# Chunk inverses of RWKV and gated delta with 32x32 diagonal blocks in four tiles of TensorE

## What is computed

```python
for i in range(DEPTH):
    xp = macaron_half(xp, *fa); xs = macaron_half(xs, *fa)
    up, us = rmsnorm(xp, norm_w[i, 1]), rmsnorm(xs, norm_w[i, 1])
    mp, ms = mixer(up), mixer(us)         # rwkv, attention, gated delta, rwkv
    xp = xp + mp; xs = xs + ms
    xp = macaron_half(xp, *fb); xs = macaron_half(xs, *fb)
```

```python
a_mat = bc[..., :, None] * einsum('nbhid,nbhjd->nbhij', kc, kc) * decay_strict + eye(L)
sol = triangular_solve(a_mat, rhs, lower=True, unit_diagonal=True)
```

## Time and profile before

| | |
|---|---|
| time, median of 3 runs | 3211.21 us (3207.57 to 3213.80) |
| the profiled execution | 3219.08 us |
| its span, first to last instruction | 3216.4 us |
| mean granted TensorE clock | 0.955 |
| PE busy | 3070.2 us, 95% of the span |
| DVE busy, ACT busy | 1532.2 us, 1066.7 us |
| FFN products, L799 to L801, six groups | 837 + 832 + 829 + 416 + 415 + 414 us |
| Y and X steps of RWKV, L1049 and L1070 | 53.4, 74.2 and 64.1 us |
| Y and X steps of gated delta, L1634 and L1658 | 13.0 and 18.9 us |

### The profile page before, as it was taken

The page is one execution under the profiler, slowest core; times in us unless marked ns, Lnnn a source line. Parts: engine busy times, 40 slices in busy tenths (PEclk is TensorE's granted clock), DMA queues, the critical chain, the costliest instruction groups (busy, mean ns, idle before and its releaser), DMA issues.

```text
span 3216.4 us, 63024 instructions
## 1 busy us (share of the span) xinstructions
PE 3070.2 (95%) x28286; PEld 2761.8 (86%) x28286; DVE 1532.2 (48%) x2422; ACT 1066.7 (33%) x1595; POOL 163.8 (5%) x266
## 2 busy tenths in 40 slices
PE   7998999999999899999999899999999999999998
PEld 6995788799999776699999767789999957887997
DVE  4644343355565204365565453446556435443554
ACT  3432232244443213244443232224344322322432
POOL 1000002100000101000000000400000000021000
PEclk9999999899999997899999899899999989997999
DMA  6442401253554634254643432155454513012532
GB/s 220 152 152 84 141 29 33 53 183 125 189 162 133 214 131 156 65 164 134 192 150 125 161 106 84 43 155 160 153 172 142 172 69 115 29 33 53 173 126 69
DMA packets 333441, 402.32 MB, mean 125 GB/s; under 512 B 14746, under 2 KB 287295, under 8 KB 332813
## 3 DMA queue, kind: packets, MB, share of 16 engines
q1 hardware_dynamic: 320176, 353.20, 33.9%
q0 software_dynamic: 13072, 46.30, 4.9%
HBM read 384.90 MB, written 14.57 MB: 124 GB/s over the span
## 4 chain that ended last, share of the span: by engine, by line
PE 92%; DVE 4%; ACT 2%; issue 1%; DMA 0%; POOL 0%; DVEq 0%; ACTq 0%; POOLq 0%
PE bank L799 18%; PE bank L801 17%; PE bank L800 17%; PE bank L832 10%; PE bank L1381 4%; PE bank L1070 2%; PE bank L908 2%; PE bank L794 2%; PE bank L868 1%; PE bank L884 1%; PE bank L1049 1%; PE bank L1023 1%; PE bank L1154 1%; PE bank L1112 1%; ACT work L1853 1%
## 5 line engine op out<-in xcount | busy, mean ns | idle before, releaser
L799 PE MATMUL bank<-h_hi,w_hi 128*128 128x288 f32 x2816 | 837.2, 297 | 5.8 <-DVE h_lo L2164 5.5
L800 PE MATMUL bank<-h_hi,w_lo 128*128 128x288 f32 x2816 | 831.5, 295 | 0.0
L801 PE MATMUL bank<-h_lo,w_hi 128*128 128x288 f32 x2816 | 828.6, 294 | 0.0
L2172 DVE TENSOR_TENSOR w_lo<-ring,w_hi 128x2048 fp32r<-128x2048 f32 (+1 forms) x304 | 611.0, 2011 | 424.3 <-ACT w_hi L1791 424.3
L1791 ACT CAST w_hi<-ring 128x2048 fp32r<-128x2048 f32 (+1 forms) x304 | 511.1, 1683 | 636.9 <-PE bank L801 568.6
L799 PEld LDWEIGHTS bank<-h_hi,w_hi 128*128 128x128 f32 x2816 | 528.3, 188 | 7.9 <-DVE w_lo L2172 6.0
L801 PEld LDWEIGHTS bank<-h_lo,w_hi 128*128 128x128 f32 x2816 | 531.0, 189 | 0.0
L800 PEld LDWEIGHTS bank<-h_hi,w_lo 128*128 128x128 f32 x2816 | 529.3, 188 | 0.6
L799 PE MATMUL bank<-hid_hi,w_hi 128*128 128x288 f32 x1408 | 416.1, 296 | 0.0
L800 PE MATMUL bank<-hid_hi,w_lo 128*128 128x288 f32 x1408 | 415.4, 295 | 0.0
L801 PE MATMUL bank<-hid_lo,w_hi 128*128 128x288 f32 x1408 | 414.3, 294 | 0.0
(11 more groups left out here) (516 smaller groups left out, 3454.2 us busy)
## 6 DMA issues: line engine op xcount, KB each, us to landing
ring<-in_ffn_w_gate SPq DMA_DIRECT2D x88, 1024.0 KB, 5.4
ring<-in_ffn_w_up SPq DMA_DIRECT2D x88, 1024.0 KB, 7.9
ring<-in_ffn_w_down SPq DMA_DIRECT2D x64, 768.0 KB, 4.6
ring<-in_ffn_w_down SPq DMA_DIRECT2D x64, 640.0 KB, 5.8
ring<-in_rwkv_w_rkv SPq DMA_DIRECT2D x24, 1024.0 KB, 7.3
ring<-in_gdn_w_in SPq DMA_DIRECT2D x16, 1024.0 KB, 6.6
ring<-in_attn_w_qkv SPq DMA_DIRECT2D x12, 1024.0 KB, 6.3
ring<-in_rwkv_w_o SPq DMA_DIRECT2D x8, 1024.0 KB, 6.3
```

Of the source, the lines that this page charges most:

```text
L799: nc.tensor.matmul(out, w_hi_k, x_hi_k, start=start, stop=False)
L800: nc.tensor.matmul(out, w_lo_k, x_hi_k, start=False, stop=False)
L801: return nc.tensor.matmul(out, w_hi_k, x_lo_k, start=False, stop=stop)
L2172: nc.vector.tensor_tensor(w_lo[e][:, 0:k, :], raw, w_hi[e][:, 0:k, :], ALU.subtract).then_inc(w_lo_ready, 1)
```

## The change

Each product of 64x64 matrices in levels 1 to 4 is replaced by products of their 32x32 diagonal blocks. In these levels the masks leave nothing outside these blocks (the block size of a level is at most 32), so the same numbers result. The four blocks in the 128 partitions (two heads, two blocks each, `QUARTERS`) go to four different tiles of PE. In level 5 only the lower left block of Y is wanted, and only the upper right block of the transpose of X: one 32x32 product for each head and step, from one quarter of the partitions into the next.

So in levels 1 to 4 the Y step has four calls where there were two, and the X step eight where there were four; in level 5 both have two as before, of 32x32 in place of 64x64. The start (L1039, L1620), the copies, the masks, all semaphores, their counts and the work between the steps stay as they are. The Y bank keeps outside the written blocks what was in it before; the mask multiplies it by zero.

```diff
+        QUARTERS = [(slice(32 * i, 32 * i + 32), 32 * (i % 2)) for i in range(4)]
...
+            def inverse_y(l, out, nt, x_):
+                if l < LADDER - 1:
+                    for r, k in QUARTERS:
+                        last = nc.tensor.matmul(out[r, k:k + 32], nt[r, k:k + 32], x_[r, k:k + 32], start=True, stop=True)
+                else:
+                    for e in range(2):
+                        upper, lower = QUARTERS[2 * e][0], QUARTERS[2 * e + 1][0]
+                        last = nc.tensor.matmul(out[lower, 0:32], nt[upper, 32:64], x_[upper, 0:32], start=True, stop=True)
+                return last
+
+            def inverse_x(l, out, y, xt):
+                if l < LADDER - 1:
+                    for w in range(2):
+                        for r, k in QUARTERS:
+                            yb, xb = y[r, k:k + 32], xt[r, k:k + 32]
+                            last = nc.tensor.matmul(out[r, 64 * w + k:64 * w + k + 32], yb if w else xb, xb if w else yb,
+                                                    start=False, stop=False, skip_group_check=True)
+                else:
+                    for e in range(2):
+                        upper, lower = QUARTERS[2 * e][0], QUARTERS[2 * e + 1][0]
+                        last = nc.tensor.matmul(out[upper, 96:128], y[lower, 0:32], xt[lower, 32:64],
+                                                start=False, stop=True, skip_group_check=True)
+                return last
...
-                            hp = 4 * g + q
-                            for r in HALVES:
-                                last = nc.tensor.matmul(bank[Y_BANK[g]][r, 64 * q:64 * q + 64], a[r, hp, 0, 64:128],
-                                                        both[r, hp, 0, :], start=True, stop=True)
+                            last = inverse_y(l, bank[Y_BANK[g]][:, 64 * q:64 * q + 64], a[:, 4 * g + q, 0, 64:128], both[:, 4 * g + q, 0, :])
...
-                            for w in range(0 if l < LADDER - 1 else 1, 2):
-                                for r in HALVES:
-                                    y, xt = Yc[r, hp, :], both[r, hp, 1, :]
-                                    last = nc.tensor.matmul(bank[X_BANK[g]][r, 128 * q + 64 * w:128 * q + 64 * w + 64],
-                                                            y if w else xt, xt if w else y,
-                                                            start=False, stop=(l == LADDER - 1), skip_group_check=True)
+                            last = inverse_x(l, bank[X_BANK[g]][:, 128 * q:128 * q + 128], Yc[:, 4 * g + q, :], both[:, 4 * g + q, 1, :])
```

More of the change, by code:

```diff
@@ L1632, in gdn_inverse @@
                         for hp in range(4):
-                            for r in HALVES:
-                                last = nc.tensor.matmul(bank[Y_BANK[g]][r, 64 * hp:64 * hp + 64], gcN[g][r, hp, :],
-                                                        gcX[g][r, hp, 0, :], start=True, stop=True)
+                            last = inverse_y(l, bank[Y_BANK[g]][:, 64 * hp:64 * hp + 64], gcN[g][:, hp, :], gcX[g][:, hp, 0, :])
                         last.then_inc(invy_raw, 1)
@@ L1654, in gdn_inverse @@
                         for hp in range(4):
[L1655 to L1660, removed]
+                            last = inverse_x(l, bank[X_BANK[g]][:, 128 * hp:128 * hp + 128], gcY[g][:, hp, :], gcX[g][:, hp, 1, :])
                         last.then_inc(inv_raw, 1)
```

## The result

The changed kernel takes 3297.22 us (median of 4 runs, 3287.46 to 3308.51), the kernel before on the same chip 3212.51 us: ratio 1.0265, with the interval 1.0226 to 1.0303. That is 85 us slower. The prediction was 3283, within 3230 to 3335. The profiled execution took 3300.74 us, its span is 3299.0.

The account below looks back on a forecast made before the run. PE bounds the kernel, and after the change its instruction packets, 3.4 us each, set the ladders' pace: +52 us from packets and +20 from a lower clock, +72, gave 3283 us, range 3230 to 3335.

Parts of the forecast that it names:

- The count: Per inverse, matmul records rise from 448 to 832, 384 more; with weight loads, 768 more PE instructions.
- The pace of the tiles: 32x32 products in the ladder issue at 8.1 ns a record, so X of both groups takes 1.04 us, now 1.89.
- the 44 us: Gain over ten inverses, 4.4 us each, from faster small products if instruction feed does not bind.
- PE's busy sum down: Sign named for a right prediction: PE's total busy time falls while the span rises; no size given.
- P: Period of PE's instruction feed, one packet per 128 matmul records with their weight loads: 3.4 us.
- the first rival: Packets do not bind PE (P under about 2.4 us, or overlapping fetches); the -44 us hold, 3167; chance 0.17.
- the 2 us of clock: Lower clock in chunk outputs and dense work behind each ladder: 2 us an inverse, +20 us in all.
- Gated delta: First inverse +7.2 us, second +1.5 as wide products make some packets slower than 3.4 us; together 8.7.
- The signs named beforehand: Issue stalls before 32x32 products, ten packets a chunk 3.4 to 3.5 us apart, chunks 36 to 40 us, clock 0.50 in ladders.
- Nothing gives it back: PE's work grows mid-path; the weight ring, fed ahead by SP, only gains time, so no added time returns.
- two cancelling limits: Rival: feed and faster tiles nearly cancel, feed period about 2.5 us, time 3211; chance 0.05.
- tiles which don't overlap: Rival: 32x32 tiles do not overlap, so PE needs more time; lies with the slower cases, no separate chance.

Follow-up runs that it names:

- one block: Changed kernel computing only the first of each head's two diagonal blocks in levels 1 to 4, 448 records per inverse: 3215.99 us, ratio 1.0012 to the kernel before.
- the run with levels 1 and 5: Changed kernel with 32x32 products only in levels 1 and 5, levels 2 to 4 as in the kernel before: 3221.47 us, ratio 1.0050.
- level 5 alone: Changed kernel with 32x32 products only in level 5, levels 1 to 4 as in the kernel before: 3199.86 us, ratio 0.9979.
- the fillers: Changed kernel plus unread dense products ending every RWKV level: ratio 1.0303; at level 4 only: 1.0258; at level 4 with twice as many: 1.0227.
- the trim of level 4: 32x32 only in level 5, plus level 4's first X product cut to its upper left block, records unchanged: 3209.46 us, ratio 0.9985 to the kernel before.

## Why the prediction held, step by step

**The count.** 384 records more per inverse: 3840 in the page. Right.

**The pace of the tiles.** Predicted 8.1 ns a record. In the windows of PE the fed stretches of X steps show it at a full clock, and chunk 0 shows what comes at half clock:

```profile
469.45:470.20 0.75, 0.75 (x93) 1.00 0.00 0
...
481.83:482.56 0.73, 0.73 (x86) 1.00 0.00 0
...
419.90:446.69 26.79, 23.60 (x875) 0.53 0.02 4
```

8.1 and 8.5 ns. The Trainium skill (TensorE: Matmul & The Clock Gate, Wait — 56ns, not 53.3ns?) has starts no closer than about 25 ns; with four tiles these rows disagree, as the earlier trace rows did. Whether the 44 us that the prediction credits to this pace would have come had the feed kept up is open: one block, the nearest run, saved 2.8 us a ladder and nothing in the total, at a pace of 20 ns a record in two tiles (X, 64 records in 1.29 us).

**"PE's busy sum down".** Wrong: it went from 3070.2 to 3074.7. The saving at a full clock was there, and the lower clock is what can have eaten it. In chunk 0 an X step and the dense L998 beside it read:

```profile
423.85 2.00 PE bank L998 x2
425.85 1.90 PE bank L1046 x128
```

128 records in 1.90 us are 14.8 ns each, in a chunk with a mean clock of 0.53. The old X step took 2.04 us there at a full clock, and L997 1.05. The step that failed is "the ladder itself, waiting for packets, would not feel it": chunk 0 hardly waited for packets (stalls of 0.70 and 0.55 us), and it felt the clock.

**The feed.** P was put at 3.4 us; from the resumption at 463.73 to that at 485.56 six packets pass in 21.83 us, 3.64 each, and the last four, in all of which PE starves, take 3.59. Of its parts, 1.05 (resumption to packet) and 1.45 (behind the packet) were right. The packet itself takes between 0.91 and 1.22 us in the four intervals shown, 1.10 on average, where I took 0.94. The Trainium skill (Runtime: NRT & Kernel Launch, Instruction fetch mechanics) holds that this fetch is hidden. These rows, in a quiet stretch, disagree, and the first rival (3167) falls with it; the run with levels 1 and 5 shows the same for a single level.

**The sum.** By terms, each inverse with the 2 us of clock I gave it. Chunks 1 to 3 are read in the two chains from the start of one tokens step to that of the next (or to the end of the ladder), chunk 0 from its first Y. The measured column is what each stretch grew by, feed and clock together:

| | predicted | measured |
|---|---|---|
| chunks 1 and 2, both layers | 21.6 + 8 | 42.7 |
| chunk 3, both | 16 + 4 | 11.2 + 9.0 = 20.2 |
| chunk 0, both | 5.4 + 4 | 4.3 + 5.0 = 9.3 |
| gated delta | 8.7 + 4 | 17.5 (stage) |
| elsewhere | 0 | -7.1 |
| span | 72 | 82.6 |

"Elsewhere" is the -6.7 of attention and the small rest. It makes the total look 7 us closer to the prediction than the stretches with inverses are: they grew by 89.7 us, where 72 was predicted.

The mis-sized term is the first. The starts of its chunks and the dense steps ahead of their ladders, with the beginning of the first as a window:

```profile
446.69:449.40 2.71, 2.71 (x52) 0.50 0.03 6
...
446.69 5.32 PE bank L1006 x96
452.00 3.57 PE bank L1024 x64
...
487.47 5.32 PE bank L1006 x96
...
2869.14 4.30 PE bank L1006 x96
```

The four ladders (from the end of the start, L1066, to the next tokens step) took 28.1, 29.1, 30.9 and 29.5 us, where 26.4 was predicted and 21.1 was before. With P at 3.64 for 3.4, 8 packets make 1.9 us more in each, 7.7 of the 12 us that are missing. The dense part ahead of the ladders took 12.6, 12.7, 12.8 and 11.6 us for 10.05, together 9.5: the clock's 8 of the prediction, though that was to cover the outputs within the ladders too. The remaining 4 us I can't assign; the outputs within the ladder at a clock of 0.5 are one candidate (L1130 x12 reads 0.64 us at some places and 0.35 at others, and five of the eight output blocks took 4.0 to 4.5 us without their stalls, 2.33 before). How much of that PE would have stood waiting for packets anyway isn't separated. The signs named beforehand are off by the same amount: the chunks took 40.8, 41.8, 43.7 and 41.0 us, not 36 to 40, and the clock in the ladders was not 0.50 throughout.

For chunk 3 the sum was right with the wrong parts, perhaps: stalls of 2.66 and 4.63 us there, and of 5.70 in the second layer, are longer than any outside of L2806's traffic, but how much is traffic and how much count wasn't taken apart, as no run moved those loads.

**Gated delta.** The first inverse was predicted at +7.2 and came at +8.5 (25.26 us from its first Y, 16.76 before). For the second I took +1.5, since its packets were sized as if the ladder's and the wide products' share one pace. It took 35.2 us from L1638 to L1685 of the next pair, 27.35 before: +7.85. The chain there shows the failed step:

```profile
2021.64 0.47 PE bank L1033 x32
...
2046.90 3.17 PE bank L1615 x32
...
2063.39 1.02 PE bank L1703 x16
...
2072.44 2.06 issue
2074.51 0.65 PE bank L1033 x32
2075.16 1.91 PE bank L1685 x16
```

The wide products (1.02 us for 16 records) and the small ones do not average out. A packet full of small products runs dry in a microsecond (128 at 8.1 ns; 2.06 us of issue follow), a packet with wide ones can be slower than P, and the time is the sum of the slower of the two for each packet. Dividing the records by 128 and multiplying by P, as I did, is a lower bound where a stretch mixes both. At 2075.16 the clock also doubles a wide step to 1.91 us, and at 2046.90 a dense one took 3.17 that took 1.90 before, so part of the gated delta's excess is clock.

**"Nothing gives it back".** Held as far as can be seen: the -6.7 us of attention come at another clock in unchanged code, and the same stage took 293.6 and 288.2 us in the runs with level 5 alone and with one block.

**The other rivals.** That of two cancelling limits and that of tiles which don't overlap are out by the rows above. The mechanism was right and its size too small: the feed takes 3.6 us a packet and not 3.4, and the clock reaches places that the prediction had left out (chunk 0, the second inverse of gated delta). How the 85 us divide between feed and clock is not shown: the tokens steps alone lost 12.8 us, but the fillers, which gave part of that back, never made the whole faster by more than its noise.

## What to carry to other kernels

Count PE's instructions before cutting a product into smaller ones: here 256 of them, or 128 matmul records with their weight loads, passed once in about 3.6 us on average where PE starved and no other transfers ran, that is 28 ns a record, and 64x64 products at 29.5 ns already stand at that edge. A cut that doubles the count cost time however fast the tiles are. One that leaves the count as it is can pay (level 5: 0.2%), but needn't: with one block computed (1.0012) and with the trim of level 4 the saving didn't arrive. And compute the feed packet by packet, never as an average over a stretch that has wide and small products in it.

## What the hardware showed that was not expected

- The clock falls in a ladder of small tiles even where PE is hardly starved: 0.90 over a chunk with PE busy for 28.09 of 29.87 us (one block), 1.00 with 64x64 products and 29.29 of 30.79 (level 5 alone). It takes 12 us in the tokens steps behind the ladders.
- With 96 records more in each inverse the kernel is 21.6 us slower, though PE's busy sum is the same (3045.5 us for 3043.8). No wait elsewhere absorbs it.
- Two dense products in a level mostly hold the clock (tokens step 2.94 us for 5.32 in four of six) and cost 1.06 us or more a level, so that a chunk takes 43.2 us for 40.8.
